# Halving the last gate units, the post-norm and the next block's first four tiles along the tokens

## The reference

```python
# end of a layer of the first block
    x = x + rms_norm(ff, norm_ffn_post[i])
    e = (p[i] @ w_ple_proj[i]) * jax.nn.sigmoid(x @ w_ple_gate[i])
    x = x + rms_norm(e, norm_ple[i])
# beginning of the next layer of the first block
    h = rms_norm(x, norm_mix_pre[i])
    z = h @ w_in[i]
    o_b = fourier_mix(h)
# beginning of the second block
    h = rms_norm_2(x, g_mix_pre[l])
    h @ w_in[l]
```

## Time and profile before

| | |
|---|---|
| median of 3 runs | 2784.98 us (2780.88 to 2787.14) |
| the profiled execution | 2785.04 us, its span 2783.2 us |
| PE busy | 2688.8 us, 97% of the span |
| DVE, ACT, POOL busy | 50%, 40%, 15% |
| granted TensorE clock, mean | 0.991 |

### The profile page before, as it was taken

The page is one execution under the profiler, slowest core; times in us unless marked ns, Lnnn a source line. Parts: engine busy times, 40 slices in busy tenths (PEclk is TensorE's granted clock), DMA queues, the critical chain, the costliest instruction groups (busy, mean ns, idle before and its releaser), DMA issues. The chain is left out here.

```text
span 2783.2 us, 34816 instructions
## 1 busy us (share of the span) xinstructions
PE 2688.8 (97%) x13520; PEld 2174.8 (78%) x13520; DVE 1399.7 (50%) x2073; ACT 1119.2 (40%) x1759; POOL 411.7 (15%) x320
## 2 busy tenths in 40 slices
PE   8999999999999899999999999999899999899997
PEld 6876778888887787677898888777687688788886
DVE  6655544533324666654453332465498536533423
ACT  6445533423224544654343222443634535522221
POOL 5100002211102310000131110231011012311101
PEclk9999999999999999999999999999999999999999
DMA  4320123132332232012322323222232222122232
GB/s 156 125 86 31 46 76 121 61 105 90 106 106 91 84 122 91 31 46 76 106 76 90 103 94 106 93 76 89 76 106 91 73 95 77 46 99 97 90 108 89
DMA packets 37501, 245.76 MB, mean 88 GB/s; under 512 B 4608, under 2 KB 5632, under 8 KB 8448
## 3 DMA queue, kind: packets, MB, share of 16 engines
q1 hardware_dynamic: 33632, 239.09, 25.3%
q10 hardware_dynamic: 3744, 4.94, 0.5%
HBM read 241.91 MB, written 2.10 MB: 88 GB/s over the span
## 5 line engine op out<-in xcount | busy, mean ns | idle before, releaser
L566 PE MATMUL bank<-h_hi,w_hi 128*128 128x512 f32 x1928 | 764.3, 396 | 7.8 <-DVEq L1603 4.3
L568 PE MATMUL bank<-h_hi,w_lo 128*128 128x512 f32 x1928 | 753.1, 391 | 0.0
L567 PE MATMUL bank<-h_lo,w_hi 128*128 128x512 f32 x1928 | 752.7, 390 | 0.0
L1565 DVE TENSOR_TENSOR w_lo<-raw,w_hi 128x2048 fp32r<-128x2048 f32 x132 | 305.5, 2317 | 347.8 <-ACT w_hi L1083 347.3
L566 PEld LDWEIGHTS bank<-h_hi,w_hi 128*128 128x128 f32 x1928 | 363.1, 188 | 95.1 <-issue 17.8
L568 PEld LDWEIGHTS bank<-h_hi,w_lo 128*128 128x128 f32 x1928 | 362.9, 188 | 76.8
L567 PEld LDWEIGHTS bank<-h_lo,w_hi 128*128 128x128 f32 x1928 | 363.4, 188 | 74.0 <-issue 1.7
L1083 ACT ACTIVATE w_hi<-raw 128x2048 fp32r<-128x2048 f32 x151 | 287.9, 1911 | 247.9 <-PE bank L568 238.6
L1577 DVE TENSOR_TENSOR w_lo<-raw,w_hi 128x2048 fp32r<-128x2048 f32 x60 | 137.6, 2293 | 156.2 <-ACT w_hi L1303 156.2
L566 PE MATMUL bank<-a_hi,w_hi 128*128 128x512 f32 x528 | 205.4, 389 | 0.0
L567 PE MATMUL bank<-a_lo,w_hi 128*128 128x512 f32 x528 | 205.4, 389 | 0.0
(11 more groups left out here) (422 smaller groups left out, 4576.0 us busy)
## 6 DMA issues: line engine op xcount, KB each, us to landing
raw<-in_stream SPq DMA_DIRECT2D x226, 1024.0 KB, 4.8
x<-in_xT SPq DMA_DIRECT2D x4, 512.0 KB, 8.6
out_T<-x ACTq DMA_DIRECT2D x8, 256.0 KB, 2.1
p_f<-in_pT ACTq DMA_DIRECT2D x2, 512.0 KB, 3.9
memf<-in_memT ACTq DMA_DIRECT2D x1, 1024.0 KB, 5.5
cst_sb<-in_cst ACTq DMA_DIRECT2D x1, 409.0 KB, 7.2
pos_i<-in_pos ACTq DMA_DIRECT2D x1, 258.0 KB, 6.0
g_in<-in_gains ACTq DMA_DIRECT2D x3, 4.0 KB, 1.6
```

The costliest lines, as they stand in the source:

```text
L566: nc.tensor.matmul(ps, wh, xh, start=start, stop=False)
L567: nc.tensor.matmul(ps, wh, xl, start=False, stop=False)
L568: return nc.tensor.matmul(ps, wl, xh, start=False, stop=stop)
L1565: nc.vector.tensor_tensor(lo[:, :], raw[v % 2][:, :], hi[:, :].bitcast(F32), ALU.subtract).then_inc(lo_ready, 1)
```

## The change

The last four tiles of `ple` are computed by halves of 256 tokens. Each PSUM bank then holds two feature tiles of one half. In the first half unit 2 comes before unit 3, in the second half unit 3 before unit 2 (`in_turn`). The post-norm, the addition to x, `raw_x_hi`, `raw_x_lo`, the squares and the next block's first four tiles follow by halves too. The unit that PE needs first of the next block goes to the separate buffer `second` (before, the second one did). The first layer's `begin` loads x by halves. The sums for the half roots are put into PE's list at chosen places.

```diff
 HALVED = {
     "wout": [2, 4, 7, 8],
+    "ple": [2, 4, 8, 7],
+    "z1a": [0, 3],
...
-            (1, "z1a"): [None, second],
+            (1, "z1a"): [second, None],
...
+        def in_turn(half):
+            return (0, 1) if half == 0 else (1, 0)
...
# PE
-            def begin(c, st):
...
+            def begin(c, st, ending=None):
...
+                for half in range(2):
+                    at = cols(half)
+                    for turn, p in enumerate(in_turn(half)):
+                        if half == 0:
+                            pe.wait_ge(lo_ready, c.at("U", st, p + 1))
+                        ps = free_bank(c, st, 2 * half + turn)
+                        hi, lo = home(c, u0 + p)
+                        for k in range(KD):
+                            if turn == 0:
+                                pe.wait_ge(raw_split, c.begun("W", KD * half + k + 1))
+                            for g in range(2):
+                                b = slice((8 * g + k) * P, (8 * g + k + 1) * P)
+                                mm = mac_at(ps[:, cols(g)], hi[:, b], lo[:, b], raw_x_hi[:, k, at], raw_x_lo[:, k, at],
+                                            k == 0 and g == 0, k == KD - 1 and g == 1)
+                            if (half, turn, k) == (0, 0, KD - 1) and ending is not None:
+                                half_sum(ending, "ple", 1)
+                            for j in (0, 1) if (half, turn, k) in ((0, 1, 6), (1, 0, KD - 1) if ending is None else (1, 1, 3)) else ():
...
+                                square_sum(sq_tree, c.begun("Q", half + 1), sq_x[:, j, at], j == 0, j == 1, ps=HALF_SS[half])
...
-                    together=0)
-                project_sum(c, "ple", sq_ready, "SQ")
+                    last=4, together=0)
+                last_units(c, "ple", lambda k, at: h_hi[:, k, at], lambda k, at: h_lo[:, k, at], 6)
# ACT
             def norm_begun(c, st, blocks):
-                for u in range(2):
-                    split_unit(c, st, u)
-                act.wait_ge(ss_done, c.at("SS", "norm1", 2))
...
+                for half in range(2):
+                    begun_root(c, half)
+                begun_hi(c, range(2))
+                split_unit(c, st, 1)
+                begun_hi(c, range(2, blocks))
...
+                for n in range(4):
+                    ple_gate(n)
+                    ple_squares(n)
+                    if n % 2 == 1:
+                        split_unit(c, "ple", n // 2)
+                ple_gate(4)
+                split_unit(c, "ple", 2)
+                ple_squares(4)
+                ple_gate(5)
                 log_table()
-                root("ple", c, 2, S, D)
+                ple_squares(5)
+                half_root(c, "ple", 0, 3, HALF_RSTD[0][:, 0:HALF])
                 act.wait_ge(gain_loaded, L * 16 + 32)
                 for m in range(KD):
-                    begin_hi(m, (x_ready, c.at("X", "post3", m + 1)))
+                    begin_hi(m, 0, (x_ready, c.at("X", "post3", m + 1)))
+                    if m % 2 == 1:
+                        begin_squares(m // 2, 0)
+                for n in (6, 7):
+                    ple_gate(n)
+                split_unit(c, "ple", 3)
+                for n in (6, 7):
+                    ple_squares(n)
+                log_table()
+                half_root(c, "ple", 1, 6, HALF_RSTD[1][:, 0:HALF])
+                split_unit(*behind(L), 0)
+                for m in range(KD):
+                    begin_hi(m, 1, (x_ready, c.at("X", "post3", KD + m + 1)))
+                    if m % 2 == 1:
+                        begin_squares(m // 2, 1)
# DVE, after the post-norm and begin_lo of half 0
+                    if half == 0:
+                        for n in (6, 7):
+                            gate_ple(n)
+                        split_unit(c, "ple", 3)
+                        add_begun(0, KD * (L + 1) + 4)
+                        split_unit(*behind(L), 0)
...
-                norm_begun(c, "z1a", cq, [("h", 0), ("h", 1), ("o", 0), ("o", 1), ("h", 2), ("h", 3), ("o", 2), ("o", 3)])
+                norm_begun(c, "z1a", cq, [("o", 0), ("o", 1), ("h", 0), ("h", 1), ("unit", 1), ("h", 2), ("h", 3), ("o", 2), ("o", 3)])
...
-            norm_begun(c, "z2", lx, [("h", 0), ("h", 1), ("o", 0), ("o", 1)] + [("h", m) for m in range(2, KD)] + [("o", 2), ("o", 3)])
+            norm_begun(c, "z2", lx, [("o", 0), ("o", 1), ("h", 0), ("h", 1), ("unit", 1)] + [("h", m) for m in range(2, KD)] + [("o", 2), ("o", 3)])
# POOL
+                        if half == 0 and m == (7 if st == "ple" else 4):
+                            half_squares(c, st, 1, ready, kind)
```

More of the change, by code:

```diff
@@ L800, in project @@
                                          i == 0 and j == 0, i == 1 and j == len(t) - 1)
-                                if half == 1 and two == 0 and i == 0 and j == 1:
+                                if half == 1 and turn == 0 and i == 0 and j == sums_at:
                                     half_sum(c, st, 0)
@@ L956, in _ @@
             c = Counts(BASE2, DEPTH)
[L957 removed]
+            begin(c, "z2", Counts(BASE1, DEPTH - 1))
             def after_z2(n):
@@ L1049, in unit_steps @@
                 for n, end in enumerate(ends):
-                    if st in SPLIT_AHEAD and n == len(ends) - 1 and end == u:
-                        split(u)
                     if end == u:
                         evac(n)
-                if u < max(ends) or st not in SPLIT_LATER and st not in SPLIT_AHEAD:
+                if u < max(ends) or st not in SPLIT_LATER:
                     split(u)
@@ L1316, in _ @@
             act.wait_ge(raw_ready[0], 16)
-            nc.scalar.activation(w_hi[0][:, :], raw[0][:, :], ACT.Copy).then_inc(hi_ready, 1)
+            nc.scalar.activation(second[0][:, :], raw[0][:, :], ACT.Copy).then_inc(hi_ready, 1)
             act.wait_ge(gain_loaded, 16)
[L1319 to L1322, removed]
+            for half in range(2):
+                for m in range(KD):
+                    begin_hi(m, half, (x_loaded[4 * half + m // 2], 16))
+                    if half == 1 and m % 2 == 1:
+                        begin_squares(m // 2, half)
+                if half == 0:
+                    act.wait_ge(raw_ready[1], 16)
+                    nc.scalar.activation(w_hi[1][:, :], raw[1][:, :], ACT.Copy).then_inc(hi_ready, 1)
+                    for m in range(KD // 2):
+                        begin_squares(m, half)
             log_table()
+            split_unit(Counts(BASE1, 0), "z1a", 0)
             def first_block(L):
@@ L2009, in first_block @@
-                post(c, "ple", "post3", 1, "ple", e, lo=lambda m: begin_lo(m, c.at("W", "begin", m + 1)))
-                add_begun(c.at("SQ", "begin", KD))
+                    if n < 4:
+                        part, by = e[:, n, :], sg[:, n % 2, :]
+                    else:
+                        half = (n - 4) // 2
+                        two = in_turn(half)[n % 2]
+                        part = e[:, 4 + 2 * two:6 + 2 * two, cols(half)]
+                        by = res[:, n - 4, :].rearrange("p (i s) -> p i s", i=2)
```

203 lines of the change are left out of this document (118 added, 85 removed).

## The result

The changed kernel takes 2802.25 us (median of 6 runs, 2798.80 to 2809.65), the kernel before 2783.23 us on the same chip (6 runs). The ratio is 1.0067, 95% interval [1.0052, 1.0083]: 0.67% slower, 19.0 us. The profiled execution took 2805.94 us, 20.9 us over that of before. The forecast was 2797.5, 12.5 us slower.

The account below looks back on a forecast made before the run. PE, busy 97% of the span, was taken as the bound, so only its waits count. Delays of 4.9 (first join), 2.4 (second), 2.9 (start) and 2.5 us (clock) sum to 12.7 over 2785.04: 2797.5 us, range 2786 to 2804.

Parts of the forecast that it names:

- Part 2: `ple` by halves at the joins: 0.9 us lost before unit 3, then `begin` starts at 25.4 without a wait.
- Part 4: Stages behind the late sums: the unit delays "h" and "o" 2; first join 4.9, second 2.4, start 2.9 us later.
- Part 1: Halved matmuls of 256 columns start 0.12 us apart: 2.6 us more per join, 1.3 us at the start.
- Part 3: Gates to sums in mid-`begin`: PE waits 1.1 us; next stage could start at 54.3, gaining 1.9 and 2.5 us.
- Part 5: Clock at the 1.2 GHz level after the waits behind both joins: 1.25 us each, bounds 0 and 2.0.
- The way round: Path through gates, squares and x in `begin`: first low part of x 1.2 us late, supply 0.89 per tile against 0.72.
- Rival A: Delay behind the late sums is absorbed, only the joins' gain and the start's 0.4 stay: 2781 us; chance 0.13.
- Rival C: Switching ACT's tables costs more than its load, delaying mid-`begin` sums: 2800 us, 2802 with the clock's upper bound; chance 0.10.
- Rival D: The hole isn't filled: PE's first sums wait on squares, `begin` starts cold as before; 2810 us; chance 0.05.

Follow-up runs that it names:

- e3: Changed kernel plus one wait: DVE's low part of `ple`'s unit 3 waits until POOL has done both additions; 2795.24 us in a single run.
- e11: The kernel of e3 measured again: 2797.76 us (4 runs), ratio 1.0055 to the kernel before.
- e12: Changed kernel with the edits of e1 and e3 together: 2781.32 us (10 runs), ratio 0.9995 to the kernel before.
- e1: Changed kernel with `norm_begun`'s weight unit moved ahead of the second half's root (ACT) and the first "h" (DVE): 2788.93 us (10 runs), ratio 1.0016.
- e4: Changed kernel with the next stage's first unit (ACT's copy, DVE's low part) moved behind the second half's x: 2797.09 us in a single run.
- e9: Changed kernel with `norm_begun`'s unit moved last, behind "o" 3 on DVE and the last rounding on ACT: 2799.09 us in a single run.
- e2: Changed kernel with ACT's squares 6 and 7 moved before the copy of `ple`'s unit 3: 2796.41 us (4 runs), ratio 1.0039.
- e7: e1, e2 and e4 together, plus `ple`'s unit 3 and gate 6 moved into the first half of x: 2782.82 us (10 runs), ratio 0.9995.
- e10: e7 with gate 6 multiplied and squared earlier, last sums after the first k, `norm_begun`'s unit placed differently for `z1a` and `z2`: 2779.14 us (11 runs), ratio 0.9982.

## Why the prediction came out as it did

The direction and most of the places were right, and the size was two thirds of what was measured. The working also has slips of 0.3 us or less: the terms of Part 2 add up to 25.1 instead of 25.4, those of `z2` in Part 4 to 69.8 instead of 70.1, and 2785.0 + 12.7 is 2797.7. In the same count (0 = 1812.90, second join):

- **Part 1** right. Matmuls of 256 columns start 0.120 us apart in after.
- **Part 2** right. At the second join unit 3 begins at 6.5, 0.8 behind unit 2's 48 matmuls (0.9 forecast), `begin` starts at 25.2 (forecast 25.4), its first half tile ends at 30.9 (31.1).
- **Part 3 is the step that failed: the term of 1.71 us for POOL's two additions was mis-sized.** They took 3.97 us. I took a row in which DVE did short operations beside POOL, and put it where my own list had DVE's 128x2048 subtraction and the sum of squares at the same time. The trace of before held a sign of it, the maximum of the same group (minimum, median, maximum in ns):

```profile
L2237 POOL TENSOR_TENSOR rstd<-rstd,sq x16: 731/777/1771, 472.5 to 2399.2; 128x256 f32<-128x256 f32 x16
```

That longest one (2388.33) begins while DVE makes a subtraction of 2.29 us (2387.21) and ends 0.60 us behind it. In after, then, the wait was 3.9 us instead of 1.1, and behind it PE ran the six sums at the 1.2 GHz level (2.37 us instead of the 1.11 counted), which Part 5 had not counted here. The sums end at 37.4 instead of 33.3: 0.6 because POOL began at 31.0 and not 30.4, 2.3 by the additions, 1.3 by the clock. The third half tile ends at 52.1 instead of 47.9. Behind the sums 13 matmuls were slow too at the first join and three at the second, yet from the first sum to the fourth half tile both take 17.1 us: the third half tile, which is short of x anyway, takes up the rest. e3 and e11 against after, and e12 against e1, show the cost of the conflict by itself: 3.0 to 3.8 us per join. The Trainium skill, "SBUF — State Buffer", section "Who interferes with whom", states the rule: a DVE instruction with two SBUF inputs contends with a GpSimd instruction that reads SBUF, the contention is an exclusive lock, and the order of issue decides who blocks. The rows above agree (POOL ends 0.59 and 0.58 us behind DVE).
- **The way round otherwise** held. The supply of x was short by 1.6 us at the second join in after: 0.56 as a wait (forecast 1.2) and 1.0 in the spacing of the third half tile (forecast 1.2), where no view shows a wait (e4).
- **Part 4** right: waits of 2.72 (2.8 forecast) and 3.03 us (3.2), and the unit is their cause (e1). What e9 adds: behind the read-outs it costs the first join as much. At the start the place came 4.1 us late instead of 2.9. PE began there at 10.95, not at the 10.5 of the forecast, and `four1` could start at 37.5 instead of 36.7; this 0.8 us is most of the difference, and the rest is open.
- **Part 5** right in the two tails (0.50 in the windows), but incomplete: the middle of both joins and the start had such a stretch too. At the start it cost little or nothing, since e2 and e11 show none there and come 4.0 us late all the same, with longer waits for `U_lo` (1.7 us instead of 0.97). One window of e11 in `four1`:

```profile
44.00:47.00 3.00, 1.27 (x10) 1.24 (x10) 1.91 (x12) 2.20 (x10) 2.59 (x3) 1.00 0.17 68
```

With the conflict taken out the forecast comes near, in part by luck. e11 is 15.1 us over the kernel before (12.5 forecast), and its first join is 6.0 us late (6.1), its second 4.7 (3.7), its start 4.0 (2.9); but in the middle of `begin` it still waits 2.3 us, where 1.1 was forecast. That its time, 2797.76 us, is next to the forecast's 2797.5 adds nothing, since the forecast counts from 2785.04 us and the kernel before took 2782.70 beside e11. So the 6.5 us between the forecast difference (12.5) and the measured one (19.0) are the conflict and its clock, 3.3 to 7.6 us by e11 and e12, and some 1 us at the start; the runs differ too much to split it further. Rival A (the tail is absorbed) did not happen; e12 shows what it takes, 1.4 us under the kernel before, where A gave 4. Rival C (a switch of tables costs more than its load) has the number that lies nearest, 2800 to 2802, but not the cause: in after the load takes 1.28 us (922.39) and the gates start at 923.68. Rival D isn't borne out either, since `begin` starts without a wait. The drain that the Trainium skill, "ScalarE: Activation LUTs", section "What ACT_TABLE_LOAD costs", puts on top of a load shows in none of these traces: each load takes 1.28 us, and at the joins the gates follow it within 0.01 us.

## What to carry to other kernels

A duration from a row belongs to its surroundings. Before an instruction of POOL is moved, look at what DVE does beside it in the new order, and look at the maximum of its group in the trace, not only at one row. One extra wait can make a kernel faster (e12 against e1, 0.2%). Where a weight conversion stands in a list can decide whether it costs anything: in three positions the same unit left the first join 9.0, 9.1 and 3.9 us late. And a PE that is fed a little too slowly can show it only in the spacing of its matmuls (0.141 instead of 0.120 us).

## What was unexpected in the hardware

- **POOL's addition and DVE's subtraction or sum don't run side by side.** The additions of 128x256 take 0.72 us alone (both of e12's at the first join) and up to 2.32 us beside DVE's subtraction of 2.29 us, while the subtraction, which began first, takes 2.29 us in e3 too, where POOL adds nothing beside it. The trace of after gives all of them:

```profile
L2345 POOL TENSOR_TENSOR rstd<-rstd,sq x24: 732/834/2323, 478.0 to 2420.1; 128x256 f32<-128x256 f32 x24
```

- **The same waits don't always bring the same clock.** In e7 `four1` starts behind waits of 1.26 and 0.52 us (946.69, 947.84), in e10 behind 1.28 and 0.51 (947.93, 949.07); the windows, first e7 and then e10:

```profile
946.00:950.00 4.00, 2.79 (x19) 2.59 (x20) 3.14 (x7) 2.60 (x6) 4.00 (x4) 1.00 0.43 180
```

```profile
949.00:952.00 3.00, 2.93 (x12) 2.93 (x13) 1.91 (x7) 1.99 (x6) 3.00 (x4) 0.50 0.68 284
```

- Nor is it a matter of this change: after waits of 0.67, 0.86 and 0.47 us in an attention stage that the change leaves alone, the clock from 380 to 384 us is 1.00 in before and 0.51 in after (first before, then after). This costs after 2.9 us there. Such places make up most of the column "elsewhere". What decides it stays open.

```profile
380.00:384.00 4.00, 4.00 (x20) 3.29 (x18) 0.09 (x1) 0.00 (x0) 0.00 (x0) 1.00 0.73 262
```

```profile
380.00:384.00 4.00, 3.52 (x16) 2.55 (x15) 2.49 (x3) 0.98 (x2) 0.00 (x0) 0.51 0.22 49
```
